# Fourier input blocks inside the differential attention's loop, and every unit piece between a step's scores and its value products

## The reference, cut to what matters

```python
def attend(q, k, v, lam):
    s = jnp.einsum('bhmqd,bhmkd->bhmqk', q, k, preferred_element_type=jnp.float32) * (B_QK ** -0.5)
    p = jax.nn.softmax(s, axis=-1)
    w = p[:, :, 0] - lam * p[:, :, 1]
    return jnp.einsum('bhqk,bhkv->bhqv', w.astype(v.dtype), v)
...
    y_b = diffattn_out(o_b, subln_w, lam_init) * jax.nn.silu(bz)
    y_c = fourier_mix(cu) * jax.nn.silu(cz)
```

## Time and profile before

| | |
|---|---|
| median of 3 runs | 2317.32 us (2316.53 to 2320.24) |
| profiled execution, span from first to last instruction | 2314.6 us |
| TensorE busy | 2220.9 us, 96% of the span |
| VectorE, ScalarE, GpSimd busy | 56%, 48%, 33% |
| attention loop of layer 1 with the last `value` | 1254.8 to 1372.1 us |
| attention loop of layer 2 | 2070.4 to 2137.7 us |

### The profile page before, as it was taken

One profiled execution on the slowest core, in us unless ns is written; L12 is line 12 of the kernel. 1 busy time (PEld: TensorE's weight loads), 2 busy tenths in 40 slices (PEclk: granted clock), 3 DMA queues, 4 the chain that ended last, 5 costly groups with the idle time before them and its releaser, 6 DMA issues.

```text
span 2314.6 us, 41122 instructions
## 1 busy us (share of the span) xinstructions
PE 2220.9 (96%) x14780; PEld 1935.8 (84%) x14780; DVE 1304.0 (56%) x2274; ACT 1112.3 (48%) x2324; POOL 764.9 (33%) x563
## 2 busy tenths in 40 slices
PE   7989998989999899999999999999989999999998
PEld 4859997868999798878878679888879999787998
DVE  3668999666445725541253764364455564437663
ACT  3565554554555535532364653232343565647553
POOL 2405874513565221112222012222213235221443
PEclk9999999999999999999999999999999999999999
DMA  8766998667766331222222113222323335222554
GB/s 303 230 219 208 322 315 301 201 210 241 237 186 196 96 91 57 64 73 91 82 74 83 35 36 94 91 73 91 99 73 110 105 116 171 83 83 65 170 162 140
DMA packets 159781, 328.47 MB, mean 142 GB/s; under 512 B 17696, under 2 KB 21024, under 8 KB 159520
## 3 DMA queue, kind: packets, MB, share of 16 engines
q1 hardware_dynamic: 159504, 325.80, 43.8%
q0 software_dynamic: 144, 0.85, 0.1%
HBM read 325.53 MB, written 1.05 MB: 141 GB/s over the span
## 4 chain that ended last, share of the span: by engine, by line
PE 65%; issue 14%; DVE 9%; POOL 5%; DMA 2%; ACT 2%; SPq 1%; POOLq 0%; ACTq 0%; DVEq 0%
PE PS L1846 13%; PE PS L1847 13%; PE PS L1848 13%; PE PS L1891 4%; PE PS L1893 4%; PE PS L1892 4%; POOL WL L1763 4%; DVE WORK L2521 3%; DVE WL L2419 2%; PE PS L729 2%; PE PS L709 1%; DMA RAW<-stream 1%; POOL AR L1783 1%; PE PS L743 1%; DMA WORK<-mods 1%
## 5 line engine op out<-in xcount | busy, mean ns | idle before, releaser
L1763 POOL TENSOR_TENSOR WL<-RAW,WH 128x512 fp32r<-128x512 f32 x434 | 618.7, 1427 | 1447.9 <-ACT WH L2158 1298.0
L1846 PE MATMUL PS<-AR,WH 128*128 128x256 f32 (+1 forms) x2632 | 857.9, 326 | 3.4 <-DVE AR L1614 1.9
L1847 PE MATMUL PS<-AR,WH 128*128 128x256 f32 (+1 forms) x2632 | 844.1, 321 | 0.0
L1848 PE MATMUL PS<-AR,WL 128*128 128x256 f32 (+1 forms) x2632 | 844.0, 321 | 0.0
L2158 ACT ACTIVATE WH<-RAW 128x512 fp32r<-128x512 f32 x840 | 490.6, 626 | 302.5 <-PE PS L1848 190.6
L2419 DVE TENSOR_TENSOR WL<-RAW,WH 128x512 fp32r<-128x512 f32 x434 | 372.5, 858 | 448.9 <-ACT WH L2158 447.2
L1846 PEld LDWEIGHTS PS<-AR,WH 128*128 128x128 f32 x2632 | 496.8, 189 | 58.8 <-issue 12.1
L1847 PEld LDWEIGHTS PS<-AR,WH 128*128 128x128 f32 x2632 | 496.8, 189 | 41.4 <-issue 2.4
L1848 PEld LDWEIGHTS PS<-AR,WL 128*128 128x128 f32 x2632 | 496.5, 189 | 40.1
L1891 PE MATMUL PS<-WH,AR 128*128 128x256 f32 x768 | 219.2, 285 | 0.0
L1893 PE MATMUL PS<-WH,AR 128*128 128x256 f32 x768 | 216.3, 282 | 0.0
(11 more groups left out here) (310 smaller groups left out, 3103.0 us busy)
## 6 DMA issues: line engine op xcount, KB each, us to landing
RAW<-stream SPq DMA_DIRECT2D x868, 256.0 KB, 3.0
WORK<-mods SPq DMA_DIRECT2D x144, 512.0 KB, 5.8
WORK<-stream SPq DMA_DIRECT2D x68, 256.0 KB, 4.7
C<-consts SPq DMA_DIRECT2D x1, 1088.0 KB, 7.4
XX<-xT SPq DMA_DIRECT2D x1, 1024.0 KB, 9.8
XX<-ctxT SPq DMA_DIRECT2D x1, 1024.0 KB, 7.7
outT<-XX SPq DMA_DIRECT2D x1, 1024.0 KB, 4.8
C<-consts POOLq DMA_DIRECT2D x1, 832.0 KB, 7.0
```

Source lines behind the costliest of these rows:

```text
L1763: pool.tensor_tensor(WL[:, u % 4, cut, :], raw(u, 1), WH[:, u % 4, cut, :].bitcast(f32), ALU.subtract).then_inc(lo_done[1], 1)
L1846: pe.matmul(out, WH[:, u % 4, k, :], moving[:, 0, k, :], start=(k == 0), stop=False)
L1847: pe.matmul(out, WH[:, u % 4, k, :], moving[:, 1, k, :], start=False, stop=False)
L1848: last = pe.matmul(out, WL[:, u % 4, k, :], moving[:, 0, k, :], start=False, stop=(k == KC - 1))
```

## The change

The stages `bz` and `cu` become one stage `bzcu` of 16 units. The weights are laid out in a new order: z0 to z3, pair c0, z4, z5, pair c1, z6, z7, pairs c2, c3. Pairs c0 and c1 go into the attention loop as single token blocks in bank 5 (`folded_block`, 24 matmuls of 256 columns), one for a step: 8 blocks in layer 1, 4 in layer 2. A block leaves the bank by one ScalarE copy to `FOLDS` (`block_copy`); VectorE folds two copies to `V2` (`block_fold`). Every piece and block now stands between `score(f + 2)` and `value(f - 1)`. Steps 1 to 29 of layer 1 all have one, and in layer 2 all steps but 0, 2, 8, 13 and 15.

```diff
+    def loop_work(l):
+        if l:
+            first_tile = {1: ("z", 1), 3: ("z", 2), 4: ("z", 3), 5: ("c", 0), 7: ("z", 4), 9: ("z", 5),
+                          10: ("c", 1), 12: ("z", 6), 14: ("z", 7)}
+        else:
+            first_tile = {1: ("z", 1), 4: ("z", 2), 7: ("z", 3), 10: ("c", 0), 14: ("z", 4), 17: ("z", 5),
+                          20: ("c", 1), 24: ("z", 6), 27: ("z", 7)}
+        out = {}
+        for f, (kind, x) in first_tile.items():
+            for part in range(len(unit_cuts(l)) if kind == "z" else per_head(l)):
+                out[f + part] = kind, x, part
+        return out
...
             def piece(x, begin, end):
-                u = st["bz"] + x
+                u = st["bzcu"] + Z_AT[x]
...
-                    if x:
+                    if x in (4, 6):
+                        pe.wait_ge(block_copied, block_count((x - 4) // 2, per_head(l) - 1, l))
+                    elif x:
                         evicted(pe, u - 1)
...
+            def folded_block(y, part):
+                u, block = st["bzcu"] + C_AT[y], 2 * l + part
+                if part == 0:
...
+                    evicted(pe, u - 1)
+                else:
+                    pe.wait_ge(block_copied, block_count(y, part - 1, l))
+                out = PS[:, 5, 0:2 * P].rearrange("p (a c) -> p a c", a=2)
...
                 if f + 2 < len(steps):
                     score(f + 2)
+                kind, x, part = loop_work(l).get(f, ("", 0, 0))
+                if kind == "z":
+                    piece(x, *unit_cuts(l)[part])
+                if kind == "c":
+                    folded_block(x, part)
                 if f:
                     value(f - 1)
                 turn(f)
-                for x, part in pieces(f, l):
-                    piece(x, *unit_cuts(l)[part])
             value(len(steps) - 1)
-            for x in range(4):
-                token_pair(st["cu"], 0, 2 * x, H2, 2 * l, 4)
-                if x in (1, 2):
-                    for h in range(4 * x - 4, 4 * x):
-                        head_turn(h)
+            for x in range(2):
+                token_pair(st["bzcu"], 0, C_AT[C_IN_LOOP + x], H2, 2 * l, 4)
+                for h in range(4 * x, 4 * x + 4):
+                    head_turn(h)
...
+            def block_copy(y, part):
...
+                act.activation(FOLDS[:, y, part, :], PS[:, 5, 0:T], ACT.Copy).then_inc(block_copied, 1)
...
                 if f + 2 < len(steps):
                     exps(f + 2)
-                for x in ended(f, l):
+                for x in z_ended(f, l):
                     z_unit(x)
+                for y, part in block_ended(f, l):
+                    block_copy(y, part)
...
+            def block_fold(y, part):
+                u, row, cut = st["bzcu"] + C_AT[y], 2 * l + part - 1, slice(y * 2 * P, (y + 1) * 2 * P)
+                dve.wait_ge(block_copied, block_count(y, part, l))
+                dve.wait_ge(pv2, tb + per * (2 * y + 2))
+                ins = dve.tensor_tensor(V2[:, row, cut], FOLDS[:, y, part - 1, :], FOLDS[:, y, part, :], ALU.add)
...
                 combine(f)
+                for x in z_ended(f - 1, l) if f else [0]:
+                    z_unit(x)
                 if f + 2 < len(steps):
                     top(f + 2)
-                for x in ended(f - 1, l):
-                    z_unit(x)
```

More of the change, by code:

```diff
@@ L269, in build @@
     FOLD, SINES = work(17408, 4, T), work(18432, 4, 2, P)
+    FOLDS = work(17408, 2, 4, T)
     VP = work(19456, 2, 2 * T)
@@ new lines, in z_ended, with block_ended, block_count, inner_count @@
+    def z_ended(f, l):
+        kind, x, part = loop_work(l).get(f, ("", 0, 0))
+        return [x] if kind == "z" and part == len(unit_cuts(l)) - 1 else []
+    def block_ended(f, l):
+        kind, y, part = loop_work(l).get(f, ("", 0, 0))
+        return [(y, part)] if kind == "c" else []
+    def block_count(y, part, l):
+        return 8 * l + per_head(l) * y + part + 1
+    def inner_count(y, part, l):
+        return 6 * l + (per_head(l) - 1) * y + part + 1
+    def high_halves(f, l):
+        out = []
+        for at in range(f + 1):
+            after = f - at - 1 + l
+            for x in z_ended(at, l):
+                out += [(Z_AT[x], after)] if after in (0, 1) else []
+            for y, part in block_ended(at, l):
+                if part == per_head(l) - 1 and after in (0, 1):
+                    out += [(C_AT[y] + after, 0), (C_AT[y] + after, 1)]
+        return sorted(out)
@@ L468, in fourier_items, with low_halves @@
+    def low_halves(f, l):
+        out = []
+        for at in range(f + 1):
+            after = f - at - 2 + l
+            out += [Z_AT[x] for x in z_ended(at, l) if after == 0]
+            for y, part in block_ended(at, l):
+                if part == per_head(l) - 1 and after in (0, 1):
+                    out.append(C_AT[y] + after)
+        return sorted(out)
     def fourier_items(l):
-        return [(p, y) for p in parts(l) for y in range(4)], 8 * l, 8 + 16 * l
+        return [(p, y) for p in parts(l) for y in range(4)], 8 * l, 4 + 16 * l
@@ L747, in piece @@
                     last.then_inc(unit_done, 1)
+            def folded_block(y, part):
+                u, block = st["bzcu"] + C_AT[y], 2 * l + part
+                if part == 0:
+                    for half in range(2):
+                        pe.wait_ge(lo_done[half], u + 2)
+                    evicted(pe, u - 1)
+                else:
+                    pe.wait_ge(block_copied, block_count(y, part - 1, l))
+                out = PS[:, 5, 0:2 * P].rearrange("p (a c) -> p a c", a=2)
+                cut, both = slice(block * P, (block + 1) * P), slice(u % 4, u % 4 + 2)
+                for k in range(KC):
+                    pe.matmul(out, H2[:, 0, k, cut], WH[:, both, k, :], start=(k == 0), stop=False)
+                    pe.matmul(out, H2[:, 0, k, cut], WL[:, both, k, :], start=False, stop=False)
+                    last = pe.matmul(out, H2[:, 1, k, cut], WH[:, both, k, :], start=False, stop=(k == KC - 1))
+                if part == per_head(l) - 1:
+                    last.then_inc(unit_done, 2)
+                else:
+                    last.then_inc(block_done, 1)
             def head_turn(h):
@@ L1144, in layer @@
             sigmoids()
-            take = halves(st["cu"])
-            for x in range(4):
+            for j in range(2):
+                evicted(act, st["bzcu"] + C_AT[0] + j)
+            take = halves(st["bzcu"] + C_AT[C_IN_LOOP])
+            for x in range(2):
                 take(2 * x)
                 take(2 * x + 1)
[L1149 to L1152, removed]
+                for k in range(4 * x, 4 * x + 4):
+                    act.wait_ge(gated, 24 * l + 8 + k + 1 + BEGUN)
+                    act.activation(Y2[:, 0, k, t0:], YB[:, k, t0:], ACT.Copy).then_inc(yhi, 1)
             merge("bmerge", 1)
@@ L2936, in _weights @@
         put(bv)
-        put(bz)
-        put(cu)
+        for first, end, y in ((0, 4, 0), (4, 6, 1), (6, 8, 2)):
+            put(bz[:, first * P:end * P])
+            put(cu[:, y * 2 * P:(y + 1) * 2 * P])
+        put(cu[:, 6 * P:])
         at_pair = np.arange(D).reshape(4, P, 2).transpose(0, 2, 1).reshape(-1)
```

57 lines of the change are left out of this document (36 added, 21 removed).

## The result

The changed kernel takes 2360.65 us (median of 4 runs, 2357.96 to 2365.46) against 2316.93 us (4 runs, 2314.22 to 2320.24). The ratio is 1.0182, with a 95% interval of 1.0167 to 1.0196: slower by 1.8%, some 42 us.

The account below looks back on a forecast made before the run. TensorE was taken to bound the kernel. The terms +2.8 - 6.1 + 34.8 + 0.3 + 2 gave +33.8 us on 2317.3, hence 2351 us, with an 8-in-10 range of 2336 to 2363 us.

Parts of the forecast that it names:

- the forecast alone: The prediction's main case for the whole kernel, without its rivals: 2343 to 2360 us, chance 0.74.
- The wait for bank 5: Attention loops: 21 joins without a free step wait until ScalarE or VectorE has emptied the bank, +34.8 us.
- the ring: Attention loops: bank 5 is freed only after turn, WT copy and two exponentials; 2.04 to 2.46 us behind a block.
- What is won: Attention loops: pieces and blocks cover turn's waits, -5.4 us in layer 1, -1.4 in layer 2, less a new wait; -6.1 us.
- the new wait of 0.7 us: End of layer 1's loop: value(29) loses its cover and waits for a WT copy, +0.7 us.
- The switches: TensorE in the loops: changing between kinds of matmul, +1.3 us for twelve blocks and +1.5 for 28 pieces, +2.8 us.
- Behind the loops: Layer 2, between the last head_turn and the merge: a pair no longer stands there, +0.3 us with handovers.
- The clock: TensorE in the loops: waits of 1.9 to 2.6 us may make the granted clock fall, +2 us, bounds 0 to 14.
- rival of no change: Bank 5's exit is no bound but the switches are paid: 2314.3 us, within 0.2%; chance 0.03.
- only the z joins wait: Rival: a block's copy is done in time, so only joins behind z units wait, 18.8 us; 2335 us, chance 0.08.
- the faster: Rival: bank 5's exit is no bound and switching matmul kinds is free, 2311.5 us; chance 0.03.
- waits as counted and more with them: Rival in the loops: ScalarE's splits delay WT copies and the clock falls at most z joins, 2361 to 2366 us; chance 0.12.

Follow-up runs that it names:

- second profile: The changed kernel run once more, unaltered: 2363.03 us, ratio 1.0196 to the kernel before.
- Experiment 1: Changed kernel with the z unit's tanh and the block's copy moved to the beginning of ScalarE's step, ahead of the WT copy: 2317.41 us, ratio 0.9989.
- experiment 4: Changed kernel with only the block's copy moved to the beginning of ScalarE's step, tanh left behind the exponentials: 2342.72 us, ratio 1.0092.
- experiment 5: Changed kernel with only the z unit's tanh moved to the beginning of ScalarE's step, block's copy left behind the exponentials: 2335.04 us, ratio 1.0074.
- experiment 6: Changed kernel with the tanh and the block's copy between the WT copy and the exponentials on ScalarE: 2320.88 us, ratio 1.0008.
- best version: Changed kernel, but layer 1 has pieces and blocks behind turn; layer 2 has tanh and block's copy first on ScalarE: 2313.13 us, again 2313.46 us.
- experiment 3: Changed kernel with blocks still in the loop, but pieces and blocks behind turn again: 2315.91 us, ratio 0.9985.

## Why the prediction was right, and what was off

The direction, the cause and the place were right. 2351 us was 10 us short of the 2360.65 measured, which is inside the range of 2336 to 2363 by 2 us and just above the 2343 to 2360 of the forecast alone. By its own steps:

- **The wait for bank 5**, +34.8 us forecast: 37.0 us in the first profile and the same in the second. Behind blocks 10.4 + 5.6 were forecast and 10.7 + 5.8 measured, behind z units 13.2 + 5.6 and 14.2 + 6.3. Experiments 1, 4 and 5 take most of the waits away by the order on ScalarE alone, and experiment 6 shows that the ring is the sum of its links. Shown.
- **What is won**, -6.1 us forecast. From the first `score` on, TensorE's idle time was 117.3 - 109.6 = 7.7 and 67.3 - 64.1 = 3.2 us; now, without the waits for bank 5, it is 165.2 - 137.5 - 24.9 = 2.8 and 91.4 - 76.8 - 12.1 = 2.5 us: -5.6 us, of which layer 2 has 0.7 where 1.4 were forecast. The lower bound of the term is off by its own words: with the new wait of 0.7 us it is -7.1 us for layer 1, not -7.8.
- **The switches**, +2.8 us forecast, is a small term that was mis-sized. TensorE's busy time in the best version, at full clock throughout, is 131.4 and 74.8 us; before it was 109.6 + 22.9 = 132.5 and 64.1 + 11.5 = 75.6. The blocks cost nothing more in the loop than outside it; the work became 1.9 us less. In layer 1 the best version has its pieces behind `turn`. Experiment 1 has TensorE's order of the changed kernel and was busy for 132.6 us there, 3.4 us of it at half clock, which leaves some 131 us at the price of half clock worked out below.
- **Behind the loops**, +0.3 us forecast: TensorE has no idle time between the loop and the merge in the changed kernel's trace; 0.
- **The clock**, +2 us forecast, is the term that was mis-sized most. In the changed kernel the same work kept TensorE busy for 137.5 - 131.4 = 6.1 us longer in layer 1 and 76.8 - 74.8 = 2.0 longer in layer 2, 8.1 us. In the second profile it was 7.6 and 5.1, 12.7 us. The prediction put it between 0 and 14 and chose near the lower end, on the strength of one wait of 2.0 us that had brought no fall. Of the nine waits of 1.9 us and more that it counted, three brought one in the first profile and seven in the second, and in each profile one more came behind a shorter wait (1.73 and 1.46 us), which it had not counted.

The sum of what the first profile shows is 37.0 + 8.1 - 5.6 - 1.9 = 37.6 us. Its span grew by 2356.2 - 2314.6 = 41.6 us, of which 3.5 us lie ahead of the first loop (it begins at 1258.3 instead of 1254.8), where the two programs do the same. Between the two loops' work both take 675.4 us. The last 0.5 us lies behind the second loop, 165.9 us for 165.4, and its cause is open. So the terms of the sum were short by only 3.8 us, partly by luck: the clock's 6.1 us too little and the switches' 4.7 us too much work against each other. The other 4.0 us of the span lie outside what the prediction added up. The median grew by 43.7 us, 2 us more than the span; runs of one kernel differ by more than that (2357.96 to 2365.46 us). The rule of the Trainium skill's page "TensorE: Matmul & The Clock Gate", Part 1, that the clock drops after an idle stretch longer than any wait here, would by itself have put the clock's term at 0. The changed kernel's windows at 0.50, where no wait was longer than 2.7 us, decide against it as the whole rule, and the same part of the page does not leave it at that: in its second failure mode short idles between groups of matmuls bring falls too, which is nearer to this trace. The example of a thin matmul on that page of the Trainium skill, in which a second PSUM buffer gave no gain, is where the prediction took its rival of no change from; the runs decide against it for this loop.

Of the rivals, "only the z joins wait" fell by the profile, and the faster and the unchanged one by the ratio. The first, waits as counted and more with them (2361 to 2366 us), is half of what happened: `value` waits for its `WT` copies as long in all as before (4.0 us in both loops), but the clock fell more often, and the time measured lies at the seam between this rival and the forecast.

## What to carry to other kernels

A buffer with one place is free when the engine that empties it gets there in its own order, not when it has time: before work is packed into every step of a loop, follow the exit of the buffer from the event that its engine waits for, through everything queued ahead of it, and hold that against what the writer does in between. If the exit stands behind a wait for something that the writer does only after it has filled the buffer (here `turn`), and the next fill holds up the next such thing, the two form a ring. Each turn of it then adds what the way to the exit is longer than the writer's other work in between, here the `score` of 0.63 to 1.06 us. Moving the emptying instruction ahead of that wait took four lines here and gave back 1.9%, and leaving the fill behind `turn` (experiment 3) did the same; filling idle steps won its few microseconds only with one or the other.

## What the runs showed of the hardware

The granted clock fell to half (0.50) in loops where no wait of TensorE was longer than 2.7 us. What it cost, from the windows above and those of experiment 4, with the time at half clock summed over slices of 0.5 us of the traces, and the work held against 131.4 and 74.8 us at full clock:

| kernel, loop | idle of TensorE, us | at half clock, us | busy beyond full clock, us |
|---|---|---|---|
| best version, layers 1 and 2 | 4.0, 2.8 | 0, 0 | 0, 0 |
| changed, layer 1 | 27.7 | 13.7 | 6.1 |
| changed, layer 2 | 14.6 | 3.4 | 2.0 |
| changed again, layer 1 | 27.7 | 17.2 | 7.6 |
| changed again, layer 2 | 14.7 | 10.2 | 5.1 |
| block's copy first, layer 1 | 17.0 | 18.4 | 7.5 |
| block's copy first, layer 2 | 8.7 | 10.2 | 4.8 |
| tanh first, layer 1 | 18.4 | 3.4 | 1.7 |
| tanh first, layer 2 | 8.7 | 0 | 0.2 |

These are the windows of experiment 4:

```profile
1255.80:1411.70 155.90, 138.94 (x791) 106.31 (x792) 92.60 (x196) 86.09 (x217) 17.88 (x14) 0.94 0.15 46
2087.50:2175.80 88.30, 79.57 (x535) 64.35 (x536) 59.23 (x112) 56.11 (x133) 17.52 (x14) 0.94 0.26 80
```

A microsecond at half clock costs 0.4 to 0.6 us of TensorE's time. How many there are does not follow from the idle time: the kernel with the block's copy first and the one with the tanh first are idle for about as long in their two loops (25.7 and 27.1 us), and have 28.6 and 3.4 us at half clock.

In the traces the two differ in the length of the single waits. With the block's copy first the long waits behind z units stay, nine of 1.97 to 2.74 us; with the tanh first they are gone but for one of 2.21 us, and twelve waits of 1.0 to 1.7 us behind blocks stay. All the profiles point the same way. The loops of the eleven have 32 waits of 1.9 us and more on TensorE, and 21 of them were followed by a fall; they have some 70 waits of 1.0 to 1.9 us, and 4 were. Each of the 25 falls began in such a wait or within 1.5 us of its end. The kernel before has one of the 32, its wait of 2.01 us, and no fall. What picks the 21 out of the 32 is open, since two profiles of one kernel do not agree on it. That the length is the cause is not shown either: no experiment changed it alone.
